# A two-layer diffusion trunk: from the seventh FFN unit on, gate and up read true normed tiles of 384 columns

## What is computed

```python
def swiglu(h, w1, w3, w2):
    return (jax.nn.silu(h @ w1) * (h @ w3)) @ w2
...
        h = rms_norm(x, norm2_g[l]) * (1.0 + sc2) + sh2
        x = x + g2 * swiglu(h, ffn_w1[l], ffn_w3[l], ffn_w2[l])
```

## Time and profile before

| | |
|---|---|
| median of 3 runs | 1115.74 us (1113.31 to 1117.57) |
| the profiled execution | 1117.22 us |
| its span | 1115.4 us |
| TensorE busy | 1066.8 us, 96% |
| VectorE, ScalarE, GpSimd busy | 497.1, 412.2, 553.4 us |
| HBM read | 162.43 MB |

### The profile page before, as it was taken

The page is one execution under the profiler, slowest core; times in us unless marked ns, Lnnn a source line. Parts: engine busy times, 40 slices in busy tenths (PEclk is TensorE's granted clock), DMA queues, the critical chain, the costliest instruction groups (busy, mean ns, idle before and its releaser), DMA issues.

```text
span 1115.4 us, 16350 instructions
## 1 busy us (share of the span) xinstructions
PE 1066.8 (96%) x6680; PEld 972.9 (87%) x6680; DVE 497.1 (45%) x953; ACT 412.2 (37%) x687; POOL 553.4 (50%) x422
## 2 busy tenths in 40 slices
PE   4799999997999999999999998899999999999997
PEld 3599899886998999999999897764899999999997
DVE  3657888238654222223333316287573232322122
ACT  0531322456324333333224244476443334333221
POOL 0364538541436555555666434203355665665662
PEclk9799999999999999999999999998999999999999
DMA  8633444456648666654656752412134444434441
GB/s 319 227 116 113 132 172 152 151 171 234 201 132 244 190 189 189 189 178 152 205 181 203 243 124 51 114 31 76 29 98 134 119 113 132 134 90 137 118 129 57
DMA packets 202054, 166.40 MB, mean 149 GB/s; under 512 B 20269, under 2 KB 184188, under 8 KB 201852
## 3 DMA queue, kind: packets, MB, share of 16 engines
q1 hardware_dynamic: 189568, 136.79, 41.1%
q10 hardware_dynamic: 12412, 28.58, 7.4%
HBM read 162.43 MB, written 2.92 MB: 148 GB/s over the span
## 4 chain that ended last, share of the span: by engine, by line
PE 80%; DVE 8%; ACT 3%; POOL 3%; DMA 3%; issue 1%; SPq 0%; ACTq 0%; DVEq 0%
PE banks L470 21%; PE banks L472 20%; PE banks L471 20%; PE banks L564 3%; POOL w_lo L1178 2%; PE banks L541 2%; PE banks L543 2%; PE banks L542 2%; PE banks L717 2%; ACT w_hi L1202 1%; PE banks L1022 1%; DVE xg_lo L1743 1%; PE banks L557 1%; PE banks L1038 1%; DMA xtok<-in_x_sample 1%
## 5 line engine op out<-in xcount | busy, mean ns | idle before, releaser
L1178 POOL TENSOR_TENSOR w_lo<-raw,w_hi 128x512 fp32r<-128x512 f32 (+2 forms) x397 | 526.7, 1357 | 544.6 <-ACT w_hi L1202 544.6
L1202 ACT ACTIVATE w_hi<-raw 128x2048 fp32r<-128x2048 f32 (+3 forms) x111 | 187.2, 1687 | 228.9 <-PE banks L472 138.7
L470 PE MATMUL banks<-xg_hi,w_hi 128*128 128x386 f32 x752 | 259.8, 345 | 1.0 <-POOL w_lo L1178 0.7
L472 PE MATMUL banks<-xg_hi,w_lo 128*128 128x386 f32 x752 | 255.0, 339 | 0.0
L471 PE MATMUL banks<-xg_lo,w_hi 128*128 128x386 f32 x752 | 254.5, 338 | 0.0
L470 PEld LDWEIGHTS banks<-xg_hi,w_hi 128*128 128x128 f32 x752 | 142.2, 189 | 10.8 <-issue 7.3
L470 PE MATMUL banks<-h_hi,w_hi 128*128 128x384 f32 (+1 forms) x424 | 146.5, 346 | 4.5 <-DVE h_lo L1715 3.2
L471 PE MATMUL banks<-h_lo,w_hi 128*128 128x384 f32 (+1 forms) x424 | 143.0, 337 | 0.0
L472 PE MATMUL banks<-h_hi,w_lo 128*128 128x384 f32 (+1 forms) x424 | 142.9, 337 | 0.0
L471 PEld LDWEIGHTS banks<-xg_lo,w_hi 128*128 128x128 f32 x752 | 142.0, 189 | 0.5
L472 PEld LDWEIGHTS banks<-xg_hi,w_lo 128*128 128x128 f32 x752 | 142.4, 189 | 0.0
(11 more groups left out here) (349 smaller groups left out, 1485.4 us busy)
## 6 DMA issues: line engine op xcount, KB each, us to landing
raw<-in_ffn_w SPq DMA_DIRECT2D x88, 512.0 KB, 5.1
raw<-in_ada_w SPq DMA_DIRECT2D x28, 1024.0 KB, 7.3
raw<-in_ffn_w SPq DMA_DIRECT2D x32, 704.0 KB, 4.6
vada_raw<-in_ada_w ACTq DMA_DIRECT2D x20, 1024.0 KB, 6.5
raw<-in_w_in_even SPq DMA_DIRECT2D x18, 1024.0 KB, 5.3
raw<-in_w_out_even SPq DMA_DIRECT2D x4, 1024.0 KB, 5.9
raw<-in_w_in_odd SPq DMA_DIRECT2D x3, 1024.0 KB, 5.4
raw<-in_w_in_odd SPq DMA_DIRECT2D x8, 256.0 KB, 4.6
```

The costliest lines, as they stand in the source:

```text
L470: pe.matmul(out, s_hi, m_hi, start=first and j == 0, stop=False)
L472: mm = pe.matmul(out, s_lo, m_hi, start=False, stop=last and j == len(terms) - 1)
L1178: ins = pool.tensor_tensor(low_part(s)[:, at:to], raw[u % RAW][:, at:to], high(s)[:, at:to].bitcast(F32), ALU.subtract)
L1202: act.activation(high(s)[:, 0:n], raw[u % RAW][:, 0:n], ACT.Copy)\
```

## The change

From unit 6 on (`TRUE_FROM`) the gate and up products of both layers read the true normed tiles, `h = X * gain * root + shift`, high and low, with 384 columns, from `h_hi`/`h_lo`. These tiles are made on the way, two k at a time, during units 0 to 4:

- VectorE, at the end of units 0 to 3 (`true_tile`): `X * gain * root` into one of two banks of `misc`, a pair of scalar_tensor_tensor for each k. The root is read from PSUM: ScalarE copies it over the sum of squares in the bank of `stat` (`root`). TensorE claims the two banks ahead of that bank, and VectorE gives back all three in unit 4.
- ScalarE, at the start of units 1 to 4, behind the split of weights (`true_high`): adds the shift and rounds into `h_hi`, a pair of Identity activations for each k.
- VectorE, at the end of units 1 to 4 (`true_low`): the low part, `true + shift - high`, a pair of scalar_tensor_tensor.

From unit 6 on ScalarE applies silu to the gate product straight out of PSUM, one activation of 384 columns; VectorE multiplies it by the up product out of PSUM, one instruction; there is no root, no shift and no pair. The u tiles move: f < 14 in `u_hi_end`, the last eight in the rows of xg, which is free by then. The tiles gained for layer 1's input projection (n = 2) go to h, whose rows grow to 400 elements for the two shift columns. The `levels` constants lose the first mask, and the scan reads the identity instead.

```diff
-        h_hi = sb("h_hi", [P, DT, T], F32R)
-        h_lo = sb("h_lo", [P, DT, T], F32R)
+        h_hi = sb("h_hi", [P, DT, TX], F32R)
+        h_lo = sb("h_lo", [P, DT, TX], F32R)
...
         def u_hi(f):
-            return h_hi[:, f, :] if f < DT else u_hi_end[:, f - DT, :]
+            return u_hi_end[:, f, :] if f < FT - DT else xg_hi[:, f - FT + DT, 0:T]
...
+        def gained_tiles(n):
+
+            return (h_hi, h_lo) if n == 2 else (xg_hi, xg_lo)
...
             def stat(n):
 
+                if n % 2:
+                    for i in range(2):
+                        misc.fill(pe, ("true", n, i))
                 out = misc.fill(pe, ("stat", n))
...
                     u = number[(f"up{l}", f)]
-                    normed(("gate", l, f), u, 0)
-                    normed(("up", l, f), u, P)
+                    if f == TRUE_FROM:
+                        pe.wait_ge(S["true_h"], DT * (l + 1))
+                    if f < TRUE_FROM:
+                        normed(("gate", l, f), u, 0, 2 * l + 1)
+                        normed(("up", l, f), u, P, 2 * l + 1)
+                    else:
+                        features(("gate", l, f), u, 0)
+                        features(("up", l, f), u, P)
...
                 act.activation(out, out, ACT.Exp, scale=-0.5).then_inc(S["rstd_ready"], 1)
+                if n % 2:
+                    act.wait_ge(S["rstd_ready"], n + 1)
+                    act.activation(bk[:, 0:T], out, ACT.Copy).then_inc(S["root_copied"], 1)
+
+            def true_high(l, m):
+
+                bk = misc.places[misc.banks[misc.at[("true", 2 * l + 1, m % 2)] % misc.n]]
+                act.wait_ge(S["true_t"], DT * l + m + 1)
+                for c, a, b in ((1, 0, TC), (0, TC, T)):
+                    ins = act.activation(h_hi[:, m, a:b], bk[:, a:b], ACT.Identity, bias=mod[:, l, 24 + m, c:c + 1])
+                ins.then_inc(S["true_hi"], 1)
...
+                    if 1 <= f <= DT // 2:
+                        true_high(l, 2 * f - 2)
+                        true_high(l, 2 * f - 1)
+                    if f < TRUE_FROM:
...
+                    else:
+                        evacuate(dense, ("gate", l, f), sa[:, i, 0:T], lambda b: b[:, 0:T], ACT.Silu)
+                        dense.was_read(act, ("up", l, f))
                     act.activation(u_hi(f), uf[:, i, 0:T], ACT.Copy).then_inc(S["uhi_ready"], 1)
...
+                def true_tile(m):
+
+                    bk = misc.filled(dve, ("true", 2 * l + 1, m % 2))
+                    if m >= 2:
+                        dve.wait_ge(S["true_h"], DT * l + m - 1)
+                    for c, a, b in ((1, 0, TC), (0, TC, T)):
+                        ins = dve.scalar_tensor_tensor(bk[:, a:b], X[:, m, a:b], gain[:, 2 * l + 1, m, c:c + 1],
+                                                       roots[:, a:b], ALU.mult, ALU.mult)
+                    ins.then_inc(S["true_t"], 1)
+
+                def true_low(m):
+
+                    bk = misc.filled(dve, ("true", 2 * l + 1, m % 2))
+                    dve.wait_ge(S["true_hi"], DT * l + m + 1)
+                    for c, a, b in ((1, 0, TC), (0, TC, T)):
+                        ins = dve.scalar_tensor_tensor(h_lo[:, m, a:b], bk[:, a:b], mod[:, l, 24 + m, c:c + 1],
+                                                       h_hi[:, m, a:b].bitcast(F32), ALU.add, ALU.subtract)
+                    ins.then_inc(S["true_h"], 1)
...
+                    else:
                         low_u(f - 1)
+                        dense.was_read(dve, ("gate", l, f))
+                        bk = dense.filled(dve, ("up", l, f))
+                        dve.tensor_tensor(uf[:, i, 0:T], sa[:, i, 0:T], bk[:, 0:T], ALU.mult)\
+                            .then_inc(dense.read(("up", l, f)), 1)
+                    if 1 <= f <= DT // 2:
+                        true_low(2 * f - 2)
+                        true_low(2 * f - 1)
+                    if f == 0:
+                        dve.wait_ge(S["root_copied"], l + 1)
+                    if f < DT // 2:
+                        true_tile(2 * f)
+                        true_tile(2 * f + 1)
...
-                    mask = lv[:, i * P:(i + 1) * P].unsqueeze(1).to_broadcast([P, H, P])
+                    mask = (lv[:, (i - 1) * P:i * P] if i else cst("ident")).unsqueeze(1).to_broadcast([P, H, P])
```

More of the change, by code:

```diff
@@ L621, in stat @@
                     mm = pe.matmul(out[:, 0:T], ones, sq[:, i, :], start=i == 0, stop=i == 1)
-                mm.then_inc(misc.done, 1)
+                mm.then_inc(misc.done, 3 if n % 2 else 1)
             def turn_y(m):
@@ L727, in gate_step @@
                     unit_ready(u)
-                    mm = three(out[0:16, 0:T], [(*weight(u, DT, k, 0, 16), h_hi[:, k, :], h_lo[:, k, :])
+                    mm = three(out[0:16, 0:T], [(*weight(u, DT, k, 0, 16), h_hi[:, k, 0:T], h_lo[:, k, 0:T])
                                                 for k in range(DT)])
@@ L1786, in low_u @@
                         .then_inc(S["u_ready"], 1)
+                roots = misc.places[misc.banks[misc.at[("stat", 2 * l + 1)] % misc.n]]
+                def true_tile(m):
[9 more added lines that the diff above has]
+                    dve.wait_ge(S["true_hi"], DT * l + m + 1)
+                    for c, a, b in ((1, 0, TC), (0, TC, T)):
+                        ins = dve.scalar_tensor_tensor(h_lo[:, m, a:b], bk[:, a:b], mod[:, l, 24 + m, c:c + 1],
+                                                       h_hi[:, m, a:b].bitcast(F32), ALU.add, ALU.subtract)
+                    ins.then_inc(S["true_h"], 1)
                 dve.wait_ge(S["rstd_ready"], 2 * l + 2)
@@ L1797, in ffn @@
[L1797 to L1801, removed]
+                    if f < TRUE_FROM:
+                        bk = dense.filled(dve, ("gate", l, f))
+                        dve.tensor_tensor(sa[:, i, 0:TS], bk[:, 0:TS], rs, ALU.mult).then_inc(dense.read(("gate", l, f)), 1)
+                        if f:
+                            low_u(f - 1)
+                        bk = dense.filled(dve, ("up", l, f))
+                        dve.tensor_tensor(uf[:, i, 0:TS], bk[:, 0:TS], rs, ALU.mult).then_inc(dense.read(("up", l, f)), 1)
+                        dense.was_read(dve, ("up", l, f))
+                        dve.wait_ge(S["silu_ready"], TRUE_FROM * l + f + 1)
+                        for c, a, b in ((1, 0, TC), (0, TC, T)):
+                            ins = dve.scalar_tensor_tensor(uf[:, i, a:b], uf[:, i, a:b], uf[:, i, T + c:T + c + 1],
+                                                           sa[:, i, a:b], ALU.add, ALU.mult)
+                        ins.then_inc(S["uf_ready"], 1)
+                    else:
+                        low_u(f - 1)
+                        dense.was_read(dve, ("gate", l, f))
+                        bk = dense.filled(dve, ("up", l, f))
+                        dve.tensor_tensor(uf[:, i, 0:T], sa[:, i, 0:T], bk[:, 0:T], ALU.mult)\
+                            .then_inc(dense.read(("up", l, f)), 1)
@@ new lines, in ffn @@
+                    if 1 <= f <= DT // 2:
[6 more added lines that the diff above has]
+                        true_tile(2 * f + 1)
+                    if f == DT // 2:
+                        dve.wait_ge(S["true_h"], DT * (l + 1))
+                        for key in (("true", 2 * l + 1, 0), ("true", 2 * l + 1, 1), ("stat", 2 * l + 1)):
+                            dve.engine_nop().then_inc(misc.read(key), 1)
```

56 lines of the change are left out of this document (28 added, 28 removed).

## The result

The change made the kernel slower by a little: 1117.34 us against 1114.58 us, medians of 20 runs each, a ratio of 1.0027 (95% interval 1.0016 to 1.0037). I had forecast 1111.2 us; on the 20-run median of before, my sum of -4.5 us would have been 1110.1. So some 7 us of what I counted on did not come.

A forecast was written before the change was run, and what follows sets the result against it. The prediction took the FFN to be bound by how fast TensorE's matmuls follow each other. From the median of 1115.74 us, 6.0 us saved on columns and 1.5 lost at layer 0's start gave 1111.2 us, range 1108.5 to 1117.

The forecast's parts named there:

- my sum of -4.5 us: Whole kernel: 6.0 us off TensorE for fewer columns, 1.5 us added at layer 0's FFN start.
- The columns term: Units 6 to 21, both layers: 1536 matmuls reading 384 instead of 386 columns save 3.9 ns each, 6.0 us.
- the lower bound of 1.3: Units 6 to 21: by the slope from 384 to 512 columns, two columns save 0.83 ns a matmul, 1.3 us.
- Even and odd k: Rows of 400 start at differing remainders of 128 bytes, yet three matmuls take 0.53 us either way; row place doesn't matter.
- rival 2: Rows of 400 carry the surplus to h and the last eight u tiles, 1248 matmuls: 1119.8 or 1122.1 us; chance 0.09.
- A term put at nothing: Moved u tiles and h replacing xg for layer 1's input projection: the same instructions, no cost.
- the start of layer 0: Layer 0's FFN: two true tiles ahead of unit 1's uf pair start unit 3 1.5 us late, between 0.5 and 4.
- Rival 1: FFN units: two columns save only 1.3 us, the rest belongs to the stage; 176.4 ns, 1115.9 us; chance 0.12.
- Rival 3: Units 1 to 4: VectorE becomes the bound if a pair into PSUM costs 1.97 us; 1121.3 us; chance 0.06.
- the lower bound of the prediction: Layer 0's FFN start: only 0.5 us lost, given a shorter low_u and pairs of 0.5 us.
- Layer 1: Layer 1's FFN start: 3.6 us of slack before unit 3 hides the true tiles, cost zero.
- the forecast's own range: Whole kernel: 1108.5 to 1114 us, from a start cost of 0.5 to 4 and 1.5 us between medians.

The follow-up runs named there:

- the pad: The changed kernel with h and the last eight u tiles in rows of 384, plus 64 bytes ahead of the stages' tiles: 1110.68 us against 1113.54, ratio 0.9971.

## Why the prediction was wrong, point by point

**The columns term is the step that failed.** "3.9 ns go with the two columns" was a difference between two layouts. Both tiles that I timed with 384 columns have rows 1536 bytes apart, a whole number of 256; xg's are 1600 apart. With rows of 400 the two columns are worth 1.1 ns, with rows of 448 at the weights' remainder 3.3, and at the best places nothing. So the term was 1536 x 1.1 = 1.7 us, near the lower bound of 1.3 that I had set aside; the stage table has 1.7 in units 6 to 21. My three reasons each fell:

- "The rows nearest to what is new are those of h itself, whose base stays": the base stayed, but the change moved every row behind the first.
- "The two tiles timed with 384 columns lie in different places and agree": they agree because in both each row starts at the same remainder of 256 bytes as the row before, and by luck: the u tiles lie 64 bytes below the weights' remainder, a place that took 173.3 ns before and 176.7 in other kernels.
- Even and odd k "would alternate": they repeat, over four k. Printed to 10 ns, three matmuls were 0.53 us each time; to the nanosecond the starts of before give 532 to 534 ns three times and then 528 or 529. 1600 bytes are 64 more than a multiple of 256, so after four rows the remainder comes back. Three rows at that resolution could not speak against rival 2.

**A term put at nothing failed with it.** "u in other tiles, h in place of xg for in1 (still 386 columns)" stood among "the same instructions". They are, but their rows are 400 elements apart, and that cost 2.1 us in the down projections and 1.0 in the mixers of layer 0. With the 4.3 us that the columns term lacked, less 0.5 at the start of layer 0, these are the 7 us that did not come.

**Rival 2 is what happened**, at another size: matmuls from h lose about 2.7 ns and not 3.1 to 3.9, but it reaches further than its 1248 matmuls: 288 token products (4 to 5 ns each), and u tiles in rows of 384 that run behind others in rows of 400. **Rival 1** had the pace right (176.4 given, 176.1 measured) and the reason wrong: nothing belongs to the stage. By the N / 2.4 + 2.5 ns that the Trainium skill (TensorE: Matmul & The Clock Gate, "Back-to-back issue gap") gives for an isolated matmul, 386 columns would cost an estimated 0.8 ns over 384; here the difference goes with the layout: 1.1 ns with rows of 400, 3.3 with rows of 448 at the weights' remainder and 0 at the best places. **Rival 3** did not come: 0.70 us a pair.

**The start of layer 0** was forecast at 1.5 us; units 0 to 3 take 0.95 us longer in the changed kernel, 1.19 with rows of 384. The low part of u between the two got shorter, 0.54 us after 0.98, which the lower bound of the prediction had named. **Layer 1** was forecast at 0, and from the output projection to unit 5 it is 0.02 us. TensorE does not wait at unit 6, as forecast.

**The median.** The sum with the term of 6.0 us is what the change does when its rows lie well: 1112.11 us, and 1110.68 with the pad. That these come near the forecast does not bear out its columns: what units 6 to 21 win there (5.4 us from unit 5 to 21 by the table) they win by their rows. And before, with its rows placed well, stands at 1106.33, its units as short (5.6 us won), without true tiles and without what they cost at the start of layer 0. One sum of the prediction does not come out: by its own terms (a start of 4 us, 1.5 us between medians) the forecast's own range ends at 1115.2 and not at 1114, which the range with rival 1 covers.

## What to carry to other kernels

Take the pace of matmuls from start to start and to the nanosecond, and before pricing columns look at where each operand's rows begin. For float32r matmuls like these, try rows of the moving operand a whole number of 256 bytes apart, and try its start against that of the weights and of the operand it alternates with, for the number of columns that you read. A difference between two tiles is not the price of the one thing in which you happen to compare them; a block of matmuls alone, one line for each layout, tells them apart in one run. When the rows of one tile change, tiles that run behind it can change their pace though their own rows stay, so time places that the edit does not name.

## What the runs showed that I had not expected

- Matmuls of 384 and of 386 columns can both run at 173.3 ns (520 ns for three, without scatter), at one pair of starts even both. Which other starts are fast depends on the number of columns.
- The pace of float32r matmuls ran from 173.3 to 180.0 ns for the same 386 columns, by the starts of the rows alone, and with 512 columns it was 226.7 or 231.7 by the rows of the stationary operand. The Trainium skill (SBUF — State Buffer, "Operand start alignment") lets an operand start at any multiple of its element size and says that this is about legality, not speed; these runs show the speed.
- Some starts have more than one pace: 384 columns 64 bytes below the weights' remainder took 173.3, 174.7 or 176.7 ns, and the u tiles of the changed kernel changed between 173.3 and 176.7 from one down tile to the next.
- Why it is so was not settled: the runs tell which places are fast, not what makes them so.
